# Transposes in place of products for the transposed partial inverse of an RWKV-7 chunk recurrence

## The reference

```python
def step(s, inp):
    r_t, w_t, k_t, v_t, kk_t, a_t = inp
    sa = jnp.einsum('bhvk,bhk->bhv', s, -kk_t)
    s = s * w_t[:, :, None, :] + sa[..., None] * (kk_t * a_t)[:, :, None, :] + v_t[..., None] * k_t[:, :, None, :]
    return s, jnp.einsum('bhvk,bhk->bhv', s, r_t)
```

## Time and profile before

| | |
|---|---|
| time, median of 3 runs | 6169.99 us (6167.9 to 6171.29) |
| span of the profiled execution, first to last instruction | 6159.2 us |
| latent recurrence, of the span | 866.9 us |
| context recurrence and state exchange | 133.1 us |
| PE / DVE / ACT / POOL busy | 4924.3 / 1753.6 / 898.5 / 494.2 us |
| mean granted clock of TensorE | 0.866 |

### The profile page before, as it was taken

How to read it: one execution, slowest core, us unless ns; L and a number is a source line. 1 busy time by engine, 2 the same in 40 slices (tenths; PEclk the granted TensorE clock), 3 DMA queues, 4 the chain that set the end, 5 groups by cost and what they waited for, 6 DMA issues and landing times. The chain is left out here.

```text
span 6159.2 us, 76147 instructions
## 1 busy us (share of the span) xinstructions
PE 4924.3 (80%) x31726; PEld 4331.8 (70%) x31726; DVE 1753.6 (28%) x2068; ACT 898.5 (15%) x1195; POOL 494.2 (8%) x284
## 2 busy tenths in 40 slices
PE   4799999963289999963516579984999999999990
PEld 1799999951189999951106434454999999999990
DVE  3200100037533333335466623334000000000006
ACT  0111111112122222212422300000000000000000
POOL 1100000003211011111101000000000000000003
PEclk6899999975589999986755789985999999999995
DMA  8422222113311111125853162225777777777755
GB/s 316 140 64 67 65 71 64 58 54 117 110 29 31 27 28 32 32 73 206 306 146 80 49 222 82 82 90 193 262 251 264 240 260 251 261 261 249 264 175 219
DMA packets 517520, 891.70 MB, mean 145 GB/s; under 512 B 149102, under 2 KB 321642, under 8 KB 498394
## 3 DMA queue, kind: packets, MB, share of 16 engines
q1 hardware_dynamic: 478596, 794.19, 38.1%
q0 software_dynamic: 5808, 38.93, 2.5%
q10 hardware_dynamic: 32964, 56.31, 2.5%
HBM read 747.98 MB, written 141.35 MB: 144 GB/s over the span
## 5 line engine op out<-in xcount | busy, mean ns | idle before, releaser
L2430 PE MATMUL ex_bank<-ex_xT,ex_ring 128*128 128x144 f32 x8192 | 1029.6, 287 | 9.5 <-DVE ex_yT L2538 9.0
L2430 PEld LDWEIGHTS ex_bank<-ex_xT,ex_ring 128*128 128x128 f32 x8192 | 1013.2, 190 | 13.8 <-issue 12.2
L379 PE MATMUL feat_acc<-proj_hH,feat_wH 128*128 128x384 f32 x2112 | 706.7, 335 | 12.6 <-DVE feat_wL L362 12.6
L379 PE MATMUL feat_acc<-proj_hL,feat_wH 128*128 128x384 f32 x2112 | 706.4, 334 | 0.0
L379 PE MATMUL feat_acc<-proj_hH,feat_wL 128*128 128x384 f32 x2112 | 706.4, 334 | 0.0
L2444 PE MATMUL ex_bank<-ex_act,ex_ring 128*128 128x144 f32 x4096 | 537.3, 297 | 0.0
L2444 PEld LDWEIGHTS ex_bank<-ex_act,ex_ring 128*128 128x128 f32 x4096 | 533.8, 200 | 0.6
L2059 PE MATMUL op_acc<-op_w,op_yT 128*128 128x512 f32 x1152 | 497.3, 595 | 25.2 <-DMA op_w<-in_w_out 25.2
L2059 PEld LDWEIGHTS op_acc<-op_w,op_yT 128*128 128x128 f32 x1152 | 219.8, 191 | 302.2 <-issue 302.2
L379 PEld LDWEIGHTS feat_acc<-proj_hH,feat_wH 128*128 128x128 f32 x2112 | 397.2, 188 | 13.0 <-DVE feat_wL L362 13.0
L379 PEld LDWEIGHTS feat_acc<-proj_hL,feat_wH 128*128 128x128 f32 x2112 | 397.3, 188 | 0.0
(11 more groups left out here) (403 smaller groups left out, 6220.9 us busy)
## 6 DMA issues: line engine op xcount, KB each, us to landing
ex_ring<-in_w_gate SPq DMA_DIRECT2D x256, 512.0 KB, 3.7
ex_ring<-in_w_up SPq DMA_DIRECT2D x256, 512.0 KB, 4.5
ex_ring<-in_w_down SPq DMA_DIRECT2D x256, 512.0 KB, 4.4
lru_wq<-in_w_mod SPq DMA_DIRECT2D x64, 1024.0 KB, 11.6
proj_raw<-in_w_in SPq DMA_DIRECT2D x43, 1024.0 KB, 5.5
mod_slab<-in_w_mod SPq DMA_DIRECT2D x8, 4096.0 KB, 31.0
scratch_FEAT<-feat_out ACTq DMA_DIRECT2D x43, 576.0 KB, 2.8
rr_bdt<-scratch_RW SPq DMA_DIRECT2D x288, 64.0 KB, 2.4
```

The costliest lines, as they stand in the source:

```text
L379: last = pe.matmul(acc[k][:, g, 0:SEG], a[:, k, t, :], b[:, t, cols], start=t == 0 and j == 0, stop=t == KT - 1 and j == 2)
L2430: last = pe.matmul(bank[b][:, n * C:(n + 1) * C], ring[:, k % RING, h * FE + f * P:h * FE + (f + 1) * P], xT[:, k, :], start=k == 0 and n ...
```

## The change

The products `Y2`, `Y4`, `Y8` and `Y16` become transposes of the new `X`, taken from its copy in SBUF with the identity as the moving operand. They wait for ACT's copy of X in place of DVE's W (and Tt or the older Y). `Y32` stays a product, since X32 is never made. The copies of Y by ACT stay.

```diff
@@ -1567,9 +1567,9 @@
 PRODUCTS = [
     ("T", "dve", ""), ("Tt", "dve", ""), ("Bt", "dve", ""), ("A2", "dve", ""), ("W2", "dve", "T Tt"),
-    ("X2", "act", "W2 Tt"), ("Y2", "act", "W2 Tt"), ("W4", "dve", "X2"), ("X4", "act", "W4 Y2"), ("Y4", "act", "W4 Y2"),
-    ("W8", "dve", "X4"), ("X8", "act", "W8 Y4"), ("Y8", "act", "W8 Y4"), ("W16", "dve", "X8"), ("vT", "act", ""),
-    ("X16", "act", "W16 Y8"), ("Y16", "act", "W16 Y8"), ("W32", "dve", "X16"), ("R", "dve", "Bt vT -S"),
+    ("X2", "act", "W2 Tt"), ("Y2", "act", "X2"), ("W4", "dve", "X2"), ("X4", "act", "W4 Y2"), ("Y4", "act", "X4"),
+    ("W8", "dve", "X4"), ("X8", "act", "W8 Y4"), ("Y8", "act", "X8"), ("W16", "dve", "X8"), ("vT", "act", ""),
+    ("X16", "act", "W16 Y8"), ("Y16", "act", "X16"), ("W32", "dve", "X16"), ("R", "dve", "Bt vT -S"),
     ("Y32", "act", "W32 Y16"), ("kT", "act", ""), ("U", "dve", "R Y32"), ("bT", "act", ""), ("Yo", "act", "U A2 vT -S"),
     ("S", "dve", "U bT kT vT"),
 ]
@@ -1720,8 +1720,10 @@
                                         last = mm(S[:, g, c, :], rt[:, slot, g, c, :], False, True, o)
+                                    elif name == "Y32":
+                                        last = mm(B("W", c), B(y, c))
                                     elif name[0] == "Y":
-                                        last = mm(B("W", c), B(y, c))
+                                        last = pe.transpose(o, B("X", c), ident[:])
```

## The result

| | before | changed |
|---|---|---|
| time, median of 4 runs each | 6170.6 us (6167.9 to 6178.4) | 6093.9 us (6092.2 to 6097.0) |
| ratio, 95% interval | | 0.9885 (0.9866 to 0.9905) |
| span of the profiled execution | 6159.2 us | 6090.3 us |
| PE busy | 4924.3 us | 4858.5 us |

The account below looks back on a forecast made before the run. The recurrence was taken as a chain bound where PE's order meets other engines' results. 0.38 us x 4 levels x 18 chunks = 27.4 us, so 6170.0 - 27.4 = 6142.6, say 6143 us; range 6133 to 6156.

Parts of the forecast that it names:

- (1) Work removed: Recurrence, PE: four of five Y groups per chunk become transposes, 0.91 us less each, 65.5 us of PE work in all.
- (2) Waits added: Recurrence levels: Y waits for ACT's copy of X; release 0.06 us, stall of 0.45 us for direction 1.
- rival B: Recurrence levels: releases of 0.25 us eat the gain, leaving 13.7 us (6156 us), or 10 us with a bubble; chance 0.07.
- (3) A level's gain: One recurrence level: W starts at 2065.15 in place of 2065.53, a gain of 0.38 us per level.
- takes 0.44 us: Recurrence levels: one direction's transposes of Y take 0.44 us on PE, against 0.89 us as products.
- (4) Other levels and engines: Recurrence: Y16 gains 0.38 us too; Y2's second wait, on DVE's mask, and the other engines cost nothing.
- (6) The clock at the turns: Latent loop's turns: clock falls lose 1.8 to 3.4 us each; change taken as zero, 5 us for the range.
- The 10.8 us: Whole kernel: the profiled span, 6159.2 us, lies 10.8 us under the median of 6170.0; taken as unchanged.
- A: Inside recurrence chunks: the clock falls, up to 2.8 us each; one per chunk gives 6193 us, slower; chance 0.06.
- C: Recurrence levels: transposes run at a quarter, 0.22 us per direction, a gain of 43 us, 6127 us; chance 0.03.

Follow-up runs that it names:

- e6: Kernel before with the four Y products made transposes of W, not of X, under the old waits, so no stall on ACT: 6067.9 us, ratio 0.9845.
- e5: Kernel before with the Y products kept as products but waiting for ACT's copy of the new X: 6163.3 us, ratio 1.0007.
- e2: Kernel before with the transposes in the 2 context chunks only, the latent loop's body unchanged: 6189.8 us, ratio 1.0042.
- e3: Kernel before with 8 idle PE instructions added at the start of the context run: 6132.9 us, ratio 0.9951.
- e1: Kernel before with the transposes in the 16 latent chunks only, the context chunks keeping their products: 6195.9 us, ratio 1.0053.
- e4: Changed kernel with 136 idle PE instructions added at the start of the context run: 6201.7 us, ratio 1.0060 to the kernel before.
- e8: Changed kernel with 136 idle PE instructions at the context run and 134 in routing, so both loops lie as before: 6140.7 us, ratio 0.9967.
- e14: Kernel before with 134 idle PE instructions added in the routing stage alone: 6221.0 us, ratio 1.0098.
- e11: Kernel before, products kept, with PE's order Y(0) W(0) Y(1) W(1) in place of Y(0) Y(1) W(0) W(1): 6155.8 us, ratio 0.9996.
- e9: Changed kernel in order Y(0) W(0) Y(1) W(1), with 145 idle PE instructions in their own block before context, 109 in routing: 6058.0 us, ratio 0.9827.
- e10: Changed kernel, order kept, with 145 idle PE instructions in their own block ahead of the context run and 109 in routing: 6097.7 us, ratio 0.9903.
- e13: Changed kernel in order Y(0) W(0) Y(1) W(1), with 146 idle PE instructions at program start and 109 in routing: 6040.5 us, ratio 0.9807.
- run 136: Not a run's label: the words "context run" followed by the count of 136 semaphore increments of PE, which cost 6.6 to 7.2 us.
- e12: Changed kernel in order Y(0) W(0) Y(1) W(1), with 175 idle PE instructions in their own block before context, 79 in routing: 6082.8 us, ratio 0.9871.

## Why the prediction was wrong

The direction and the mechanism inside a level were right; what failed was the part on the turns of the loop.

- **(1) Work removed** (65.5 us). Right: in e6, without a stall, a Y group goes from 1.79 to 0.88 us (2029.39 to 2030.27). PE's busy time fell by 65.8 us, but that holds the slow matmuls at the turns too and is no clean measure.
- **(2) Waits added.** Right: direction 1's stall is 0.47 us (0.45 forecast) and the release 0.05 us (0.06 taken), far from the 0.25 us of rival B. e5 and e6 show it alone: the wait costs 0.06 us a level behind a product and 0.47 us behind a transpose. Wrong in the first of the four levels: its second wait, taken as free because DVE's mask was long done, makes the release 0.11 us, in e5 too.
- **(3) A level's gain**, 0.38 us. A little low: 0.44 us in three of the four levels, and 0.38 us in the first, by its longer release. Counted from X's load, the forecast has the two transposes, W and the next X at 1.86, 2.75, 3.19 and 5.21 us; the rows above have 1.84, 2.74, 3.12 and 5.14. So 0.06 of the 0.07 us are in the term "takes 0.44 us": four transposes that start afresh after the stall take 0.38 us to the next load. The step from W to the next X is 2.02 us as before, mask stall and all, as forecast. The 72 levels give 27.3 + 3.4 = 30.7 us in place of 27.4.
- **(4) Other levels and engines** at nothing. Right for ACT, DVE, POOL and SP. Not thought of: PE's own instruction stream, which became 136 instructions shorter ahead of the latent loop and 270 ahead of the experts.
- **(6) The clock at the turns.** This is the step that failed: "I take zero and 5 us for the range". It took the two idle times for given and only asked how long the clock stays low behind them. The second one, with "issue" as its reason, was nobody's wait for a result, and that was the sign that it could go. It went, with the clock's fall: 35.0 us, more than the levels gave. e2 and e3 have it without any change to the loop, e1, e4 and e8 have the change without it. Some 31 us of the 35 are the place alone (e2, e3). The other 4 need both: with the old loop at the new place the clock still fell at two turns, with the changed loop at none, and why is open.
- **The 10.8 us** between span and median, taken as unchanged, give the last 7.8 us of the difference. That the forecast also erred here has nothing to do with the change.
- **Luck.** That the changed kernel came out faster than forecast, and not slower, is luck of placement: nothing in the prediction or the change aimed at it.

Put together for the profiled spans: 27.3 (levels, latent) + 35.0 (turns, the latent run's remainder) + 4.5 (context) + 2.1 (the other stages, each under 1.5) = 68.9 us.

**The rivals.** A is refuted: the clock is 1.00 in the whole latent run, though every level now has 0.88 us of transposes and a stall. The Trainium skill's page TensorE: Matmul & The Clock Gate (Part 4), by which transposes do not count as activity, would have let one fear for the clock; with products for the rest of each level, it cost nothing here. B is refuted by the release. C too: a group of four took 0.38 to 0.44 us, not 0.22. That page's factor of four for FP32 transposes (Terms) was two again.

A chance was missing: that the whole gain is doubled, or lost, by something outside the change's own lines. It could have been lost: had the change shifted the experts by 134 in place of 270, it would have been slower than before, as e1, e2 and e4 were. How the changed kernel would fare at every other placement was not measured; the ones tried span 6093.9 (as it stands) to 6201.7 us (e4).

## What to carry to other kernels

Here an idle time of PE at the turn of a hardware loop with "issue" as its reason was a fetch of instructions; the instruction queue in the DMA view tells. Where it is one, count the loop's instructions and those ahead of it before pricing any edit that changes their number, in later stages' loops too. Compare two versions at the same placement, or with idle instructions that restore it, before a gain or loss is put down to the edit. A product that becomes a cheaper operation exposes the copy it covered; put the other direction's next product into that gap (31 us here, about 7 us before the change).

## What the runs showed of the hardware

**Code loading at the jump back.** PE's stream is fetched in blocks of 16 KB, 256 instructions (rows of the instruction queue). A loop of PE that touches 8 blocks or more was fetched whole in every turn, in the latent loop with an idle time of 1.5 to 2.1 us just behind the jump, in the experts' loop with one of 2.0 to 4.3 us (e1, e2, e4, e14). In the latent loop another of 1.8 to 3.3 us followed, with a fall of the clock at nearly every turn, where the body begins just ahead of a block's edge (before, e1, e4, e5, e8, e11, e14). "Whole" is one block more than the loop touches: 10 for nine, 9 for eight. Loops that touch 7 were fetched once (e9, e10, e13; the experts of before). The price of the fetches, with single idle times, was 14 to 20 us over 7 turns of the latent loop and 54 to 70 us over the experts' turns. The Trainium skill's page Runtime: NRT & Kernel Launch (Instruction fetch mechanics) gives TensorE room for 2048 instructions in blocks of 256, calls the crossing of a block mostly hidden, and warns of taken branches whose target lies outside a window of two blocks. The block size agrees, and the warning too; the window does not: a jump back over 1682 instructions, over six blocks, cost no fetch. That 8 blocks of room keep a loop of only 7 agrees with the runs if one block is always being filled ahead; that is argued, not shown.

**Two waits at once.** Where direction 1's transposes wait for ACT alone, PE loads 0.05 us behind the end of the copy; where they wait for ACT and DVE, 0.11 us, though DVE was long done (changed kernel, first level of a chunk).

**Idle instructions are not free.** Ahead of the context run 136 semaphore increments of PE cost 6.6 to 7.2 us (e8, e4), 145 and a block of their own 11.5 to 12.7 us (e9, e10), 175 and the block 15 us (e12); at the start of the program 146 cost nothing that could be measured (e13).

**The same fetches, different prices.** Nine fetches a turn cost the experts 59.9 us in e1, 70.3 in e2, 67.2 in e4 and 54.5 in e14. PE's idle time explains 37.3, 40.7, 38.0 and 35.6 us of that; the rest, 22.6, 29.6, 29.2 and 18.9 us, is longer busy time for the same matmuls at a mean granted clock of 0.94 to 0.95 in place of 0.96. Without fetches too the clock moved that stage: 1780.1 us in e9, with PE busy for 1737.7 us in place of 1729.2.

**Left open.** Why the idle time at the experts' jump is longer than at the latent loop's, and which turns see the clock fall behind a single idle time, was not followed up; and why a jump within kept blocks shows no idle time at all was not tried apart.
